# A hybrid diffusion backbone on one core: the tensors of the SBUF placed in another order

## The reference, cut to what matters

```python
h   = rms_norm(x, g_mix) * (1 + scale) + shift           # the "normed activations"
p   = split(h @ w_in)                                    # three groups of heads
mix = concat(neighbourhood_attention(p), mlstm(p), latent_attention(p)) @ w_out
x   = x + gate1 * mix                                    # the residual
h   = rms_norm(x, g_ffn) * (1 + scale2) + shift2
a, b = split(h @ w_ffn_in)
x   = x + gate2 * ((silu(a) * b) @ w_ffn_out)            # D_FF = 2816
```

## Time and profile before

| | |
|---|---|
| median of 3 runs | 2223.57 us (2223.35 to 2224.59) |
| the profiled execution | 2229.28 us, span 2227.5 us |
| PE busy | 2092.5 us, 94% |
| PE weight loads busy | 1721.1 us, 77% |
| DVE, ACT, POOL busy | 54%, 34%, 29% |
| granted TensorE clock, mean | 0.978 |
| DMA | 74 GB/s over the span |

### The profile page before, as it was taken

One profiled execution on the slowest core, in us unless ns is written; L12 is line 12 of the kernel. 1 busy time (PEld: TensorE's weight loads), 2 busy tenths in 40 slices (PEclk: granted clock), 3 DMA queues, 4 the chain that ended last, 5 costly groups with the idle time before them and its releaser, 6 DMA issues.

```text
span 2227.5 us, 30035 instructions
## 1 busy us (share of the span) xinstructions
PE 2092.5 (94%) x11738; PEld 1721.1 (77%) x11738; DVE 1200.1 (54%) x2143; ACT 751.1 (34%) x1221; POOL 644.7 (29%) x820
## 2 busy tenths in 40 slices
PE   7888999989989999999999998889998979999998
PEld 4777788866667888888888877778866657888886
DVE  7467513567885776177537566653368854212111
ACT  4333323456663211111111234423265643212221
POOL 1210311220002343334333430131220014555555
PEclk9999989999999999999999999998899999999999
DMA  7300432110002233233223310021110002322322
GB/s 289 105 15 29 142 110 69 38 48 10 10 10 67 76 130 116 76 114 136 91 95 116 102 50 10 20 69 39 38 48 20 10 19 76 95 95 95 98 96 100
DMA packets 76242, 165.58 MB, mean 74 GB/s; under 512 B 5192, under 2 KB 46664, under 8 KB 75088
## 3 DMA queue, kind: packets, MB, share of 16 engines
q1 hardware_dynamic: 75728, 163.28, 22.0%
q10 hardware_dynamic: 384, 0.47, 0.1%
HBM read 161.63 MB, written 2.10 MB: 74 GB/s over the span
## 4 chain that ended last, share of the span: by engine, by line
PE 79%; DVE 11%; issue 4%; ACT 4%; PEld 1%; POOL 1%; DMA 0%; PEldq 0%; DVEq 0%; SPq 0%; ACTq 0%; POOLq 0%
PE psum L1097 22%; PE psum L1099 21%; PE psum L1098 21%; PE psum L1696 1%; DVE naptlo L2105 1%; PE psum L1148 1%; PE psum L1726 1%; PE psum L1336 1%; PE psum L1465 1%; PE psum L1451 1%; PE psum L1402 1%; DVE maplo L2356 1%; PE psum L1221 1%; PE psum L1189 1%; POOL wlo L539 1%
## 5 line engine op out<-in xcount | busy, mean ns | idle before, releaser
L539 POOL TENSOR_TENSOR wlo<-raw,whi 128x256 fp32r<-128x256 f32 x816 | 644.5, 820 | 1572.5 <-ACT whi L564 1572.5
L1097 PE MATMUL psum<-hhi,whi 128*128 128x512 f32 (+1 forms) x1640 | 589.0, 359 | 16.8 <-DVEq L1899 8.6
L1098 PE MATMUL psum<-hlo,whi 128*128 128x512 f32 (+1 forms) x1640 | 579.3, 353 | 0.0
L1099 PE MATMUL psum<-hhi,wlo 128*128 128x512 f32 (+1 forms) x1640 | 578.8, 353 | 0.0
L564 ACT ACTIVATE whi<-raw 128x1024 fp32r<-128x1024 f32 x204 | 215.7, 1059 | 877.3 <-PE psum L1099 870.9
L1097 PEld LDWEIGHTS psum<-hhi,whi 128*128 128x128 f32 x1640 | 312.9, 191 | 73.2 <-issue 18.8
L1099 PEld LDWEIGHTS psum<-hhi,wlo 128*128 128x128 f32 x1640 | 312.5, 191 | 42.7
L1098 PEld LDWEIGHTS psum<-hlo,whi 128*128 128x128 f32 x1640 | 313.0, 191 | 40.5 <-issue 0.2
L2538 DVE TENSOR_TENSOR ffuf<-ffsa,psum 128x768 f32<-128x768 f32 (+1 forms) x44 | 36.1, 821 | 313.0 <-ACT ffsa L1047 306.2
L2523 DVE SCALAR_TENSOR_TENSOR ffmacc<-wm,csil,ffmacc 128x256 f32<-128x256 f32 x336 | 188.3, 601 | 10.4 <-DVE ffmacc L2523 5.3
L1097 PE MATMUL psum<-uhi,whi 128*128 128x512 f32 (+1 forms) x528 | 189.1, 358 | 3.5 <-DVE ulo L2542 1.9
(11 more groups left out here) (331 smaller groups left out, 3401.0 us busy)
## 6 DMA issues: line engine op xcount, KB each, us to landing
raw<-w_stream SPq DMA_DIRECT2D x204, 512.0 KB, 3.7
wm<-w_mod SPq DMA_DIRECT2D x80, 512.0 KB, 4.2
wm<-w_mod SPq DMA_DIRECT2D x8, 1024.0 KB, 13.1
xres<-x_t SPq DMA_DIRECT2D x8, 384.0 KB, 7.1
out<-xres SPq DMA_DIRECT2D x8, 256.0 KB, 3.2
consts<-c_f SPq DMA_DIRECT2D x1, 353.0 KB, 3.4
narpb<-rpb ACTq DMA_DIRECT2D x2, 120.0 KB
mlmask<-c_gate ACTq DMA_DIRECT2D x2, 108.0 KB
```

The source lines that it names most:

```text
L539: nc.gpsimd.tensor_tensor(wlo[:, q % 2, c:c + UW // 4], raw[:, q % RAW, c:c + UW // 4], whi[:, q % 2, c:c + UW // 4], ALU.subtract).then_i ...
L1097: mm(dst, ah, bh, start=first, stop=False)
L1098: mm(dst, ah, bl, start=False, stop=False)
L1099: return mm(dst, al, bh, start=False, stop=last)
```

## The change

The block that creates the PSUM tensor, the bank helpers, the scope functions and the scopes is moved up, right behind `hhi` and `hlo`. As scopes close again, a placeholder `scopes` of `SCOPES` elements (97,664 bytes, as long as the longest scope, the ring) then holds their region, and `xres`, `raw`, `whi`, `wlo`, the constants and all the small tensors follow it. No instruction is added, removed or moved on any engine: only the addresses in them differ. `hhi` and `hlo` go down by 24,576 bytes, the shared region by 65,984 bytes, `xres` up by 146,816 bytes, and everything from `raw` on up by 97,664 bytes.

```diff
 RING_AT = 20832
+SCOPES = RING_AT + RING * UW + 512
...
-        xres = sb("xres", [P, KT, TOK])
         hhi = sb("hhi", [P, KT, TOK], fp32r)
         hlo = sb("hlo", [P, KT, TOK], fp32r)
+        psum = es.enter_context(nc.psum_tensor("psum", [P, 8 * 512], fp32))
...
+        RNG, NRM, NA, ML, MA, FF = (scope(f) for f in (ring_scope, norm_scope, na_scope, ml_scope, ma_scope, ff_scope))
+        sb("scopes", [P, SCOPES])
+        xres = sb("xres", [P, KT, TOK])
         raw = sb("raw", [P, RAW, UW])
         whi = sb("whi", [P, 2, UW], fp32r)
         wlo = sb("wlo", [P, 2, UW], fp32r)
...
         tab = sb("marope", [P, SEQ])
-        psum = es.enter_context(nc.psum_tensor("psum", [P, 8 * 512], fp32))
...
-        RNG, NRM, NA, ML, MA, FF = (scope(f) for f in (ring_scope, norm_scope, na_scope, ml_scope, ma_scope, ff_scope))
```

More of the change, by code:

```diff
@@ L199, in build @@
         RNG, NRM, NA, ML, MA, FF = (scope(f) for f in (ring_scope, norm_scope, na_scope, ml_scope, ma_scope, ff_scope))
+        sb("scopes", [P, SCOPES])
+        xres = sb("xres", [P, KT, TOK])
+        raw = sb("raw", [P, RAW, UW])
+        whi = sb("whi", [P, 2, UW], fp32r)
+        wlo = sb("wlo", [P, 2, UW], fp32r)
+        consts = sb("consts", [P, 3 * P + 256 + 64 + 2])
+        ident = consts[:, 0:P]
+        ones = consts[:, P:2 * P]
+        ones2 = consts[:, 2 * P:3 * P]
+        band = consts[:, 3 * P:3 * P + 256]
+        colmask = consts[:, 3 * P + 256:3 * P + 320]
+        msel = consts[:, 3 * P + 320:3 * P + 322]
+        identb = sb("identb", [P, P], bf16)
+        dirmask = sb("dirmask", [P, 2, P], bf16)
+        lc = sb("lc", [P, DEPTH, NCOL])
+        mods = sb("mods", [P, DEPTH, 48, 2])
+        amix = sb("amix", [P, DEPTH, 2, KT, 2])
+        cin = sb("cin", [P, KT, 2])
+        csil = sb("csil", [P, KT, 32])
+        eps = sb("eps", [P, 1])
+        stat = sb("stat", [P, 2, 8])
+        tab = sb("marope", [P, SEQ])
         def norm_bufs(l, which):
```

## The result

| | before | after |
|---|---|---|
| median of 6 runs each | 2223.01 us (2218.40 to 2224.59) | 2237.68 us (2234.05 to 2242.64) |
| ratio of the times, 95% interval | | 1.0072 (1.0057 to 1.0087) |
| profiled execution, span | 2229.28, 2227.5 us | 2236.98, 2235.2 us |

The changed kernel is 14.7 us slower by the medians (interval of the ratio: 12.7 to 19.3 us). 2237.68 lies just outside the range of 2202 to 2237. The spans differ by 7.7 us only, since the execution profiled of before was one of its longer ones; so I compare distances between starts, not the two spans. Lines are two further down in the kernel after (`mm3` is L1099, L1100, L1101).

The account below looks back on a forecast made before the run. TensorE was taken to bound the kernel, by matmul count times distance between starts. Gains of 3.1 and 0.4 us summed to 3.5 us, taking the median from 2223.57 to 2220.1 us, with an 8-in-10 range of 2202 to 2237.

Parts of the forecast that it names:

- What bounds the kernel: FFNs and projections: TensorE busy 94% of the span; time is the number of matmuls times the distance between starts.
- That placement sets the distance: fp32r matmuls on TensorE: operand start addresses set the distance between starts, in steps of 6.7 ns; height of moving operand irrelevant.
- The first rival: Whole kernel: the two levels belong to the code, not the address, so nothing changes; 2223.6 us, chance 0.15.
- The modulus: Long TensorE streams: a moving operand 64 bytes off a multiple of 128 runs at another level than one on it.
- two forms: Moving operand: either its address modulo 128 alone counts, or its distance to the weights modulo 128.
- Point 3: Matmuls with `hhi`, `hlo`: starts stay on a multiple of 128, so zero taken for 3120 of 512 and 1800 of 256 columns.
- Part 1: FFN streams with `uhi`, `ulo`, put on a multiple of 128: 3.5 us gained, 0.4 us lost, net 3.1 us gained.
- Part 2: Shorter streams: `cqhi`, `cqlo`, `naohi`, `naolo`, `ckhi` gain, `mlo`, `maphi` lose; 0.4 us gained.
- Part 4: DVE, ACT and POOL work and DMAs at other addresses: zero taken; 1% on the chain would be 2.5 us either way.
- The rival that came true: Streams with `hhi`: distance modulo 256 or the weights' height counts and hurts; 2232 or 2244 us, chance 0.20.
- its 2232: Slower rival on `hhi` streams: 20.8 us lost at 512 columns, 12.0 us gained at 256, so 8.8 us lost.
- Its 2244: Slower rival on `hhi` streams without the gain at 256 columns: 20.8 us lost at 512 columns.

Follow-up runs that it names:

- five kernels: The changed kernel (1.0072) and four against before: weights high at distance 0 (0.9984), two small tensors moved (1.0037), shared region moved (0.9995), `cin` moved (1.0041).
- 28 bytes: Kernel before with `hhi`, `hlo`, `uhi`, `ulo` all starting 28 bytes further on than the weights modulo 256: 2204.81 us, ratio 0.9906.
- the two kernels that had it: Kernel before with 64 bytes of padding ahead of the shared region: 0.9995; changed kernel with `cin`, `stat` moved ahead of `raw`: 0.9984 to before.
- the two tensors ahead of `raw`: Kernel before with `cin` and `stat` (64 bytes each) moved ahead of `raw`, weights staying low: 2230.79 us, ratio 1.0037.

## Why the prediction was wrong

**What bounds the kernel: right.** In the long streams the time is the number of matmuls times their distance, and the four terms land inside the measured intervals of five kernels.

**That placement sets the distance: right.** The first rival, nothing changes, is refuted by rows and time. The Trainium skill's rule in "TensorE: Matmul & The Clock Gate", "Step-by-step: what each phase is for", that loading the next weights takes nothing from the running matmul, is not borne out for fp32r here: moving the loaded operand alone by 64 bytes took a matmul of 512 columns from 226.7 to 233.3 ns, and the four distances spread by 6.8 ns with 128 columns loaded and by 0.8 ns with 32. That the moving operand's height doesn't matter was right too (`hhi` at byte 41,088 and at 16,512, both at distance 0: 227.8 and 227.7 ns), and for the weights it is now shown.

**The modulus: wrong, and this is the step that failed.** I took the 64 bytes by which `uhi` was off as a matter of modulo 128, in two forms of which I wrote that for this change both say the same. A third form, the distance modulo 256, fitted the same rows as well, and for this change it says something else; I had it only as a rival. Point 3 then took nothing for the 3120 matmuls of 512 columns with `hhi`. They cost 4.8 ns more each, 15.0 us.

**Part 1, `uhi` (3.1 us gained): right about what distance 0 gives, wrong that the change leads there.** The gain is that of distance 0, and the rows of the kernel with the shared region alone moved gave 3.4 us of it. The change leads to distance 128 instead: 0.8 us gained at 512 columns, 2.2 lost at 256.

**Part 2 (0.4 us gained) was not settled**: the streams concerned are short. The three 512-column groups lie at 232.7 (cq), 232.0 (na) and 232.9 (`mlo`) after, against 233.2, 232.8 and 229.7, so about 0.2 us lost at this width. **Part 4, zero, was right**: 819, 1059 and 751 ns.

**The rival that came true was given 0.20 and the wrong price.** Its mechanism, in the form of the distance, is what happened. I had priced it with the two levels that before showed, 233.3 and 113.3, as if every distance but 0 were the same. Distance 128 is a level of its own: 232.6 at 512 columns, 15.0 us of the 20.8 priced, and 119.2 at 256, so that the 12 us given back at 256 columns, on which its 2232 rested, did not come. Its 2244 without that gain was 6 us too high, its 2232 6 us too low.

**Could it have been seen?** Before's long streams held two distances only, 0 and 192, and after has neither. The rows could not give the third level, but they could say that it was unknown, and for most of the chain. The evidence for modulo 128 was `mlo`, and that lies at 128 modulo 256 just like the weights: it spoke for modulo 256 as well. The preference for the form that leaves the largest term at zero had no row behind it.

## What to carry to other kernels

Where TensorE streams fp32r with a weight load beside every matmul, write down the distance modulo 256 between the streamed and the loaded operand before and after any change of placement, even one of 64 bytes ahead of them. A distance that the old trace doesn't hold has an unknown price. A kernel of matmuls alone gives an estimate in one run, good to about 1 ns for `hhi` here but up to 4 ns off for `uhi`, so the whole kernel has the last word. Here 28 bytes were worth 0.9% of the whole kernel. Distance 0 for all long streams was worth 3.7 us by the rows, under 0.2%, and 0.05% and 0.16% by the times of the two kernels that had it.

## What was new about the hardware

- In streams of fp32r matmuls with 128 columns loaded for each, the distance between starts goes from 226.7 to 240.0 ns at 512 columns and from 113.3 to 123.3 at 256, by placement alone, at full clock. The two widths don't favour the same distance: at 0 it is 226.7 and 120.0, at 192 it is 233.4 and 113.3 or 117.8.
- Distance 0 runs evenly (226 and 227 ns in turn, in the run of the earlier trace rows); distance 128 doesn't (228 to 241 ns in the `hhi` run shown of after).
- Starts 8 bytes apart can differ by 13.3 ns a matmul (distances of 244 and 252 bytes: 240.0 and 226.7).
- Weights at byte 204,288 (after) are as good as weights at 106,752 (the two tensors ahead of `raw`): 232.6 ns for `hhi` with both, at distance 128.
- With 32 or 64 columns loaded instead of 128 the order of the distances changes: at 512 columns distance 0 is the best of the four with 128 loaded (226.7 ns) and the worst with 32 (231.6).
- Open: why `uhi` ran at 114.7 ns for 256 columns at distance 192 and at 229.2 for 512 at distance 64, where matmuls alone at the same places modulo 256 gave 117.8 and 233.3 (there the low parts lie an odd multiple of 256 bytes behind the high ones, in the whole kernel an even one, and no run separates that); why the stream keeps 231 ns at 512 columns with 32 columns loaded; why 28 bytes are good; and why the short 512-column runs of the latent attention, where `hhi` is the loaded operand, stand at 232.3 before at distance 0 as well.
